# Expert results added to the residual in HBM by accumulating indirect DMAs, against scattering them on TensorE

## The reference, cut to what matters

```python
logits = (t @ w_router).astype(jnp.float32)
top_vals, top_idx = lax.top_k(logits, TOP_K)
gates = jax.nn.softmax(top_vals, axis=-1)
comb = jnp.einsum('nk,nke->ne', gates, jax.nn.one_hot(top_idx, N_EXPERTS, dtype=jnp.float32))
y = jnp.zeros_like(t)
for e in range(N_EXPERTS):
    y = y + comb[:, e:e + 1].astype(t.dtype) * swiglu(t, wg[e], wu[e], wd[e])
return y.reshape(B, S, D)
```

## Time and profile before

| What | Value |
|---|---|
| Three runs | 1994.24, 1990.9, 1994.18 us; median 1994.18 |
| The profiled execution | 1993.76 us; span from its first to its last instruction 1991.9 us |
| Busy share of the span | PE 98%, DVE 71%, ACT 59%, POOL 4% |
| Granted TensorE clock | 0.993 of full speed over the span |
| DMA over the span | 500.87 MB, mean 251 GB/s |
| Experts stage | from about 1183 us to the end |

### The profile page before, as it was taken

One profiled execution on the slowest core, in us unless ns is written; L12 is line 12 of the kernel. 1 busy time (PEld: TensorE's weight loads), 2 busy tenths in 40 slices (PEclk: granted clock), 3 DMA queues, 4 the chain that ended last, 5 costly groups with the idle time before them and its releaser, 6 DMA issues.

```text
span 1991.9 us, 27573 instructions
## 1 busy us (share of the span) xinstructions
PE 1953.0 (98%) x9292; PEld 1625.6 (82%) x9292; DVE 1405.2 (71%) x1665; ACT 1178.0 (59%) x1501; POOL 80.5 (4%) x104
## 2 busy tenths in 40 slices
PE   9989999999999999999998989999999999999998
PEld 7778888888888888888887878888888888888886
DVE  8766654644554454546666668989998989898996
ACT  7656544434434343435555657777777777777774
POOL 8200000000000000000200000000000000000000
PEclk9999999999999999999999999999999999999999
DMA  9544566566656656665654549999999999999996
GB/s 354 150 136 150 180 191 188 191 191 190 189 190 189 190 185 198 189 185 187 188 168 136 166 146 369 344 370 347 371 348 375 343 372 345 369 347 371 346 370 245
DMA packets 137235, 500.87 MB, mean 251 GB/s; under 512 B 15424, under 2 KB 15440, under 8 KB 135728
## 3 DMA queue, kind: packets, MB, share of 16 engines
q1 hardware_dynamic: 135440, 488.74, 71.7%
q0 software_dynamic: 1696, 10.86, 1.4%
HBM read 495.33 MB, written 4.20 MB: 251 GB/s over the span
## 4 chain that ended last, share of the span: by engine, by line
PE 87%; DMA 4%; DVE 3%; ACT 3%; POOL 2%; issue 2%; DVEq 0%; SPq 0%; ACTq 0%; POOLq 0%
PE main L546 27%; PE main L548 27%; PE main L547 27%; DMA raw_pieces<-in_ffn_moe 3%; DVE w_low L1297 1%; PE spread L889 1%; ACT w_high L972 1%; PE spread L890 1%; PE transpose L876 1%; PE transpose L915 1%; PE transpose L564 1%; PE transpose L745 0%; PE transpose L857 0%; DVE heads_scratch L1345 0%; DVE small L1346 0%
## 5 line engine op out<-in xcount | busy, mean ns | idle before, releaser
L1297 DVE TENSOR_TENSOR w_low<-raw_pieces,w_high 128x1024 fp32r<-128x1024 f32 x919 | 1095.1, 1221 | 419.4 <-ACT w_high L972 415.3
L972 ACT ACTIVATE w_high<-raw_pieces 128x1024 fp32r<-128x1024 f32 x919 | 941.9, 1058 | 248.6 <-DMA raw_pieces<-in_ffn_dense 124.5
L546 PE MATMUL main<-w_high,xT_high 128*128 128x512 f32 (+1 forms) x1920 | 734.8, 383 | 2.2 <-DVE w_low L1426 1.3
L548 PE MATMUL main<-w_high,xT_low 128*128 128x512 f32 (+1 forms) x1920 | 723.4, 377 | 0.0
L547 PE MATMUL main<-w_low,xT_high 128*128 128x512 f32 (+1 forms) x1920 | 722.5, 376 | 0.0
L546 PEld LDWEIGHTS main<-w_high,xT_high 128*128 128x128 f32 x1920 | 363.3, 189 | 67.0 <-issue 2.1
L548 PEld LDWEIGHTS main<-w_high,xT_low 128*128 128x128 f32 x1920 | 362.6, 189 | 66.9
L547 PEld LDWEIGHTS main<-w_low,xT_high 128*128 128x128 f32 x1920 | 363.3, 189 | 62.8
L546 PE MATMUL main<-w_high,hT_high 128*128 128x512 f32 x832 | 329.1, 396 | 0.0
L548 PE MATMUL main<-w_high,hT_low 128*128 128x512 f32 x832 | 324.6, 390 | 0.0
L547 PE MATMUL main<-w_low,hT_high 128*128 128x512 f32 x832 | 324.2, 390 | 0.0
(11 more groups left out here) (229 smaller groups left out, 954.7 us busy)
## 6 DMA issues: line engine op xcount, KB each, us to landing
raw_pieces<-in_ffn_moe SPq DMA_DIRECT2D x528, 512.0 KB, 5.3
raw_pieces<-in_ffn_dense SPq DMA_DIRECT2D x264, 512.0 KB, 3.6
raw_pieces<-in_w_in SPq DMA_DIRECT2D x96, 512.0 KB, 3.6
raw_pieces<-in_w_out SPq DMA_DIRECT2D x32, 512.0 KB, 3.6
x_resid<-in_x SPq DMA_DIRECT2D x4, 512.0 KB, 14.9
xn_rows<-token_major POOLq DMA_DIRECT2D x2, 1024.0 KB, 5.2
out_x<-x_resid SPq DMA_DIRECT2D x8, 256.0 KB, 2.6
token_major<-in_x_t SPq DMA_DIRECT2D x1, 1024.0 KB, 9.4
```

The costliest lines, as they stand in the source:

```text
L546: pe.matmul(out_ap, lh[ls], rh[rs], start=first, stop=False)
L548: return pe.matmul(out_ap, ll[ls], rh[rs], start=False, stop=last)
L972: act.activation(WH[:, piece % RING, :], RAWS[:, piece % RING, :], ACT.Copy).then_inc(high_done, 1)
L1297: dve.tensor_tensor(WL[:, piece % RING, :], RAWS[:, piece % RING, :], WH[:, piece % RING, :], ALU.subtract).then_inc(low_done, 1)
```

## The change

The residual is stored to a new HBM tensor `residual_rows` of 256 + 128 rows, behind `xn_rows` on POOL: both tiles, and one more time the first tile into the 128 rows behind them, so that every row of the tensor is written once. For experts 0 to 6, ACT copies each down block, times the slot's gate, from PSUM to an SBUF tensor `Y` (slots x 2048) and frees the bank with that. Once all four are copied, POOL issues one indirect DMA of 128 rows of 8 KB that adds `Y` to the rows of the slots' tokens; slots without a token add to the 128 rows at the end. The scatter on PE, the low part and the sums on DVE, and the transposed selection stay for expert 7 alone, whose selection is transposed at steps 13 and 15. In expert 7, POOL loads the residual back in four column blocks of 512 KB, after steps 8, 17, 26 and 35, and each of expert 7's sums waits for its block.

The matmul of step 12 now has three columns (token number, gate, 1), and DVE makes of them the index of the gather, the gate and the row of the result, with four small instructions in place of one; two small copies at step 8 hand them on (ahead of them, DVE waits for the accumulation of the expert before the last finished one), and one more picks the three columns. This also runs once ahead of expert 0, where PE waits for it after the first 8 pieces. POOL waits for the last accumulation before it issues the next. The second pass keeps the old way. The core of the diff:

```diff
-E_SELT = {62: 0, 63: 1}
+E_SELT, E_SELT_LAST = {62: 0, 63: 1}, {13: 0, 15: 1}
+E_BACK = {8: 0, 17: 1, 26: 2, 35: 3}
@@ POOL
             pool.wait_ge(rows_stored, 16 * (TILES + 1))
+            pool.wait_ge(dn_free, FFN[1]["dn"])
+            for t in range(TILES):
+                pool.dma_start(RESULTS[t * P:(t + 1) * P, :], X[:, t, :]).then_inc(x_out, 16)
+            pool.dma_start(RESULTS[SEQ:SEQ + SLOTS, :], X[:, 0, :]).then_inc(y_out, 16)
+            pool.wait_ge(x_out, 16 * TILES)
+            pool.wait_ge(y_out, 16)
             for e in range(N_EXP - 1):
-                pool.wait_ge(idx_done, e + 1)
+                pool.wait_ge(idx_done, e + 2)
                 pool.indirect_dma_start(XG, None, ROWS[:, :], bass.IndirectOffsetOnAxis(ap=IDX[:, 0:1], axis=0)).then_inc(xg_in, 16)
+                pool.wait_ge(y_out, 16 * e + 16)
+                pool.wait_ge(cur_done, e + 1)
+                pool.wait_ge(dn_free, PASS[0]["dn"] + DBLOCKS * (e + 1))
+                pool.indirect_dma_start(RESULTS[:, :], bass.IndirectOffsetOnAxis(ap=RC[:, 0:1], axis=0), Y, None,
+                                         compute_op=ALU.add).then_inc(y_out, 16)
             pool.wait_ge(xg_in, 16 * (N_EXP - 1))
+            pool.wait_ge(y_out, 16 * N_EXP)
+            for i, d in E_BACK.items():
+                pool.wait_ge(used, PASS[0]["piece"] + (N_EXP - 1) * SLICE_PIECES + 8 + i)
+                pool.dma_start(X[:, :, d * NB:(d + 1) * NB],
+                               RESULTS[0:SEQ, d * NB:(d + 1) * NB].rearrange("(t p) n -> p t n", p=P)).then_inc(back_in[d], 16)
@@ PE, expert(e, more)
                         if i == E_INDEX and more and n_pass == 0:
-                            slot_tokens(e)
+                            pe.wait_ge(sel_done, e + 2)
+                            pe.wait_ge(idx_done, e + 1)
+                            slot_values()
-                        if i in E_SCATTER:
+                        if i in E_SCATTER and (n_pass or not more):
                             scatter(e, *E_SCATTER[i])
@@ ACT, expert(e, more), at E_DOWN_END
+                            if more and n_pass == 0:
+                                if d == 0:
+                                    act.wait_ge(cur_done, e + 1)
+                                act.activation(Y[:, d * NB:(d + 1) * NB], DN[d % 2][:, :], ACT.Copy,
+                                               scale=GC[:, 0:1]).then_inc(dn_free, 1)
+                            else:
                                 act.activation(YH[d % 2], DN[d % 2][:, :].rearrange("p (c n) -> p c n", n=P), ACT.Copy).then_inc(y_high, 1)
@@ DVE
+                def slot_values(count):
+                    dve.tensor_scalar(IDX[:, :], U[0][:, 0:1], float(SEQ), None, ALU.add)
+                    dve.tensor_copy(GN[:, :], U[0][:, 1:2])
+                    dve.tensor_scalar(PLACE[:, 3:4], U[0][:, 2:3], PLACE[:, 1:2], PLACE[:, 2:3], ALU.mult, ALU.add).then_inc(place_done, 1)
+                    dve.wait_ge(place_done, count)
+                    dve.tensor_tensor(RN[:, :], U[0][:, 0:1], PLACE[:, 3:4], ALU.add).then_inc(idx_done, 1)
@@ DVE, expert(e, more)
+                    direct = n_pass or not more
+                        if i == E_SELECT and not direct:
+                            dve.wait_ge(y_out, e * 16 + 16)
+                            dve.tensor_copy(GC[:, :], GN[:, :])
+                            dve.tensor_copy(RC[:, :], RN[:, :]).then_inc(cur_done, 1)
-                        if i - 1 in E_DOWN_END:
+                        if i - 1 in E_DOWN_END and direct:
                             low_of_down(e, E_DOWN_END[i - 1])
-                        if i - 2 in E_SCATTER:
+                        if i - 2 in E_SCATTER and direct:
                             scattered(e, *E_SCATTER[i - 2], more)
@@ DVE, scattered, pass 0
+                        dve.wait_ge(back_in[d], 16)
```

More of the change, by code:

```diff
@@ L137, with expert_selt, expert_groups @@
 E_SCATTER = {44: (0, 0), 46: (0, 1), 49: (1, 0), 50: (1, 1), 55: (2, 0), 56: (2, 1), 60: (3, 0), 61: (3, 1)}
-E_SELT = {62: 0, 63: 1}
+E_SELT, E_SELT_LAST = {62: 0, 63: 1}, {13: 0, 15: 1}
 E_SELECT, E_INDEX = 8, 12
+E_BACK = {8: 0, 17: 1, 26: 2, 35: 3}
 D_TURN = {10: 0, 18: 1, 26: 2, 34: 3, 42: 4, 45: 5}
-def expert_groups(more):
+def expert_selt(more, n_pass):
+    if n_pass:
+        return E_SELT if more else {}
+    return {} if more else E_SELT_LAST
+def expert_groups(more, n_pass):
     tp, high = {}, {}
     for i in range(SLICE_PIECES):
-        for kind, at in (("t", E_TURN), ("gather", E_GATHER), ("st", E_SELT)):
-            if i in at and (more or kind == "t"):
+        for kind, at in (("t", E_TURN), ("gather", E_GATHER if more else {}), ("st", expert_selt(more, n_pass))):
+            if i in at:
                 tp[kind, at[i]] = len(tp)
@@ L184, in trunk @@
     PASS = []
-    for _ in range(PASSES):
-        PASS.append(dict(piece=n_piece, gu=n_gu, dn=n_dn, tp0=n_tp, tp=n_tp + KD // 4 + TILES,
-                         high0=n_high, high=n_high + KD // 4, silu=n_silu, sc=n_sc))
+    for n_pass in range(PASSES):
+        tp_more, high_more = (len(v) for v in expert_groups(True, n_pass))
+        tp_last, high_last = (len(v) for v in expert_groups(False, n_pass))
+        n_st = TILES if n_pass else 0
+        PASS.append(dict(piece=n_piece, gu=n_gu, dn=n_dn, tp0=n_tp, tp=n_tp + KD // 4 + n_st, tp_more=tp_more,
+                         high0=n_high, high=n_high + KD // 4, high_more=high_more, silu=n_silu, sc=n_sc))
         n_piece += N_EXP * SLICE_PIECES
@@ L365, in trunk @@
         idx_ready, idx_done, xg_in = sem("idx_ready"), sem("idx_done"), sem("xg_in")
+        val_done, cur_done, place_done = sem("val_done"), sem("cur_done"), sem("place_done")
+        x_out, y_out = sem("residual_stored"), sem("y_out")
+        back_in = [sem(f"back_in{d}") for d in range(DBLOCKS)]
         sel_done = sem("sel_done")
@@ L416, in _ @@
                 sp.wait_ge(sc_free, 2 + n_sc)
-            last = PASS[0]["sc"] + (N_EXP - 1) * SC_EXPERT
+            last = PASS[0]["sc"]
             for d in range(DBLOCKS):
@@ L859, in gather, with slot_values @@
                     ins.then_inc(tp_ready, 1)
-                def slot_tokens(e):
-                    pe.wait_ge(sel_done, e + 2)
-                    pe.wait_ge(sc_free, e * SC_EXPERT + 2)
+                def slot_values():
                     for t in range(TILES):
-                        ins = pe.matmul(U[0][:, 0:1], SEL[:, t, :], TOKEN[:, t:t + 1], start=t == 0, stop=t == TILES - 1)
+                        ins = pe.matmul(U[0][:, 0:3], SEL[:, t, :], VCUR[:, t, :], start=t == 0, stop=t == TILES - 1)
                     ins.then_inc(idx_ready, 1)
@@ L892, in expert @@
                 def expert(e, more):
[L893 to L894 removed]
+                    tp, _ = expert_groups(more, n_pass)
+                    tp_e, TP_MORE = s["tp"], s["tp_more"]
+                    selt = expert_selt(more, n_pass)
                     for i in range(SLICE_PIECES if more else NEXT_GU):
@@ L948, in moe_pass @@
                     gate_up(0, j)
-                for t in range(TILES):
-                    selection_transposed(s["tp0"] + KD // 4 + t, s["tp0"] + KD // 4 + t, t)
+                if n_pass:
+                    for t in range(TILES):
+                        selection_transposed(s["tp0"] + KD // 4 + t, s["tp0"] + KD // 4 + t, t)
+                else:
+                    pe.wait_ge(val_done, 1)
+                    slot_values()
                 with pe.Fori(0, N_EXP - 1) as e:
@@ L1245, in expert @@
                 def expert(e, more):
-                    tp, _ = expert_groups(more)
+                    tp, _ = expert_groups(more, n_pass)
+                    TP_MORE = s["tp_more"]
                     for i in range(SLICE_PIECES if more else NEXT_GU):
@@ L1667, in expert @@
                                               ALU.mult).then_inc(gu_free, 1)
+                        if i == E_SELECT and not direct:
+                            dve.wait_ge(y_out, e * 16 + 16)
+                            dve.tensor_copy(GC[:, :], GN[:, :])
+                            dve.tensor_copy(RC[:, :], RN[:, :]).then_inc(cur_done, 1)
                         if i == E_SELECT and more:
+                            if not direct:
+                                dve.tensor_copy(VCUR[:, :, :], VAL[:, :, :, bass.ds(e + 1, 1)].rearrange("p t k o -> p t (k o)"))
                             select(bass.ds(e + 1, 1))
-                        if i == E_INDEX + 2 and more and n_pass == 0:
-                            dve.wait_ge(idx_ready, e + 1)
-                            dve.tensor_scalar(IDX[:, :], U[0][:, 0:1], float(SEQ), None, ALU.add).then_inc(idx_done, 1)
-                        if i - 1 in E_DOWN_END:
+                        if i == E_INDEX + 2 and not direct:
+                            dve.wait_ge(idx_ready, e + 2)
+                            slot_values(e + 2)
+                        if i - 1 in E_DOWN_END and direct:
```

(12 more changed lines are left out.)

62 lines of the change are left out of this document (42 added, 20 removed).

## The result

The changed kernel takes 1996.22 us in the median of 14 runs (1991.76 to 1999.13), the kernel before 1991.97 us (14 runs, 1987.23 to 1994.24). The ratio is 1.0026, with a 95% interval of 1.0018 to 1.0035: slower by about 4 us, where 20 us less were forecast. The profiled execution took 1999.13 us, the longest of the 14.

What follows compares the result with a forecast made beforehand. PE was taken as the bound, with DVE and DMA right behind; -29.4 + 7.5 + 0.3 + 0.6 + 1.0 = -20.0 us gave 1974 us, forecast range 1966 to 1986, 8-in-10 range 1964 to 2003.

Steps and rivals of the forecast that it cites:

- The place and the mechanism: Block 0's transpose, experts 1 to 7: delayed loads make `h_blocks` late; beyond about 4 us PE stalls one for one.
- The price of the accumulation: DMA time of one accumulation: 5.2 us, twice a gather's 2.6, for two reads; bounds 2.6 to 10.5 us.
- What the change removes: Scatter groups and two selection transposes on PE: 4.2 us for each of experts 0 to 6, 29.4 us in all.
- DVE's wait for the landing: At step 8 DVE waits for the accumulation; landing in 10 to 15 us passes, beyond some 25 it hurts.
- the stores at the start: 3 MB of stores ahead of the experts delay the loads by 3.5 to 4 us: +0.3 us, bounds 0 to 4.
- its term of 7.5 us: Accumulation's cost in experts 1 to 7: 7 x 0.9 us at block 0's transpose plus 6 x 0.2 behind it.
- the slack: At block 0's transpose, about 4 us of load delay are free; a delay of 4.9 us stalls PE by 0.9.
- the prediction's chain: Piece 13's high part to `h_blocks` in expert 2: ready at 1403.9 plus the delay, against PE's arrival at 1407.77.
- my sum of -20.0: Whole kernel, in us: -29.4 + 7.5 + 0.3 + 0.6 + 1.0, giving 1974 us.
- Rival 2: At the transposes: accumulation costs three gathers, 7.9 us; stalls of 25 us give the saving back, 1993 us; chance 0.11.

Runs made afterwards that it cites:

- the plain store: The changed kernel with the seven indirect DMAs storing their rows and not adding them; 1967.93 us, ratio 0.988 to the kernel before.
- the floor: The changed kernel without the seven accumulating DMAs, so the results of experts 0 to 6 aren't added; 1966.97 us, ratio 0.9871 to the kernel before.
- the filler: The changed kernel with 20 transposes of the identity on PE ahead of the wait for block 0 in every expert; 1987.89 us, ratio 0.9987.
- The two groups put back: The changed kernel with four matmuls into an unread bank at steps 60 and 61 of experts 0 to 6; 1989.03 us, ratio 0.9983.
- the eight groups: The changed kernel with matmuls for all eight scatter groups of experts 0 to 6 at their old steps, into an unread bank; 2013.02 us, ratio 1.0094.
- the halves: The changed kernel with the residual in two HBM tensors of 1024 columns and each accumulation in two of half the size; 1973.74 us, ratio 0.9913.

## Why the prediction was wrong

**Right, and borne out.** The place and the mechanism: loads delayed by the accumulation, `h_blocks` behind the low part of piece 14, PE waiting at block 0's transpose in each of experts 1 to 7, one for one beyond a slack. The price of the accumulation: 5.3 us against 5.2, and 2.5 for the plain store. The Trainium skill (Collectives: The Full Stack, Part 3) halves the rate of a reduce-scatter because an add needs two source reads; twice a copy's price agrees with this case's trace, which shows the price and not the reads. What the change removes: 4.2 us for an expert was forecast, and the floor shows 94.9 us against 99.5. DVE's wait for the landing never bit (11.2 to 11.8 us against some 25 allowed), nor did the stores at the start (no wait of PE over 0.3 us from expert 0's first weight matmul to 1258 us). With no accumulation the kernel gains 23 us on the kernel before beside it; my sum without its term of 7.5 us is 27.5, less the 2.9 of the setup that it left out.

**The step that failed** is the slack: "It meets 1407.77 at D = about 4." I read PE's arrival and the loads from the trace of before and moved only the loads. But the two scatter groups at steps 60 and 61 and the two selection transposes stood between the issue of the late loads and PE's arrival, 0.9 + 0.24 us, and the change takes these away too. PE arrives earlier by what it was spared. The two timelines show it when both are counted from ACT's copy of the last down block (1390.44 and 1391.70). PE reaches block 0's transpose 17.33 us behind it before and 16.13 after (1407.60 + 0.23): 1.2 us earlier. Piece 13 lands 9.40 us behind it before and 14.60 after: a delay of 5.2 us and not 4.9. `h_blocks` is ready 18.52 us behind it, as the prediction's chain has it (13.46 + 5.2 = 18.7). So the slack in the changed kernel is below 3 us, and 0.9 us becomes 2.4; the mean measured is 2.6. Seven stalls cost 18.0 us and not 6.3. The two groups put back (2.6 to 1.9 us) show the effect, and the eight groups (1.8 us left of a delay of 5.2 to 5.3) put before's own slack at about 3.5 us, or 3.7 with its two selection transposes, an estimate, and not 4.

**Terms that weren't in the sum.** (1) The clock: a stall doesn't only cost its own length. Six drops at 1.7 us are 10.2 us, shown by the filler. (2) POOL's setup: seven instructions ahead of the rope tables, 2.9 us. I had followed the accumulation through POOL's queue and not the constants that it needs, though the diff has them in `masks`. With the stalls' 11.7 us, the clock's 10.2 and these 2.9 on top, my sum of -20.0 becomes +4.8; measured were +4.3.

**The ledger of the experts:** from expert 0's first weight matmul to the end the kernel without accumulation takes 770.9 us, 29.8 less than before. 18.0 of them come back as stalls at block 0, 10.2 as clock drops, and the other 1.6, by my reading, in small waits of expert 0 and expert 7: zero, as the profiled spans say. Rival 2 (given back at the transposes) came nearest, with the right place and the wrong cause: not a dearer accumulation but less slack and the clock.

**Open.** 2.3 of the 5.2 us ahead of the experts lie in the second mixer and the router, where the clock stood low for longer in this execution (20.4 us against 13.6 between 1050 and 1195 us). No experiment was made on them. They may be the execution's own: in the seven other profiles that have the setup early, and the same work ahead of the experts but for how the stores are cut in the halves, the first weight matmul starts at 1192.4 to 1195.0 us and not at 1196.4.

## What to carry to other kernels

When work is taken off the engine that sets the pace, work out the slack of the late transfers anew: every instruction removed between a load's issue and its use was part of that slack. Split a large background transfer, or place it where the pacing engine has other work; the same bytes cost 22 us less in two pieces. And price a stall of TensorE with the clock that it may lose, not by its length alone.

## What was not expected of the hardware

- An indirect DMA that adds 128 rows of 8 KB to HBM beside a full stream of loads held the DMA engines for 5.3 us, against 2.6 us for a gather and 2.5 us for a plain store of the same size, and the stream stood nearly still meanwhile: 6.8 us between two pieces that otherwise land 1.3 us apart.
- In the midst of a stage in which PE was busy for 97% of the time, waits of 2.2 to 3.1 us were followed in six of seven cases by 3.4 us at 1.2 GHz. The length doesn't decide alone: the wait of 3.05 us in expert 1 had none, nor did 2.25 and 2.45 us with two groups back, while there 2.06 us had one, and with all groups back 1.88 and 1.84 us had one each.
- More work on PE made the kernel faster, twice: by 7 us with four matmuls that compute nothing of use, and by 8 us with 20 transposes.
